# Norm sums on TensorE tile by tile, the scale spread from its column, and four column tiles per pass at the start of both attentions

## The chip, the cores and the metric

The kernel runs on one core of a Trainium2 chip. The metric is the time of one execution on the device in microseconds, lower is better. Three runs of the kernel before took 2327.4, 2330.2 and 2330.41 us, so its median is 2330.2 us. The profiled execution is a run of its own.

## The reference, cut to what matters

The model takes x of 512 positions by 1024 channels and runs three blocks after each other: a conformer convolution with a gated MLP, a differential attention with a gated MLP, and a block with two attention branches (a sparse one with top-k selection and a latent one) and an MLP. Only the norms and the products at their borders matter here.

```python
def rms_norm(x, g):
    y = x32 * lax.rsqrt(jnp.mean(x32 * x32, axis=-1, keepdims=True) + EPS)
    return (y * g.astype(jnp.float32)).astype(x.dtype)
...
h = rms_norm(x, norm_g[l, 0]) * (1.0 + sc_m) + sh_m
y = conformer_conv(h, ...)            # inside: layer_norm over channels
x = x + g_m * rms_norm(y, norm_g[l, 1])
h = rms_norm(x, norm_g[l, 2]) * (1.0 + sc_f) + sh_f
y = conv_ffn(h, ...)
x = x + g_f * rms_norm(y, norm_g[l, 3])
...
hkv = rms_norm(x, kv_norm_g)
k_shared, v_shared = hkv @ w_k, hkv @ w_v
```

A norm needs, for each position, the mean of squares over 1024 channels, its inverse root r, and then every channel of that position times r.

## The kernel before, in words

**Layout.** Channels lie on the 128 partitions and positions in the free dimension, so x is 8 tiles of 128x512 (`XT`). A mean over channels is a sum over partitions and over the 8 tiles. All large products are made of three products of split operands: `mm3` (L280 to L283) multiplies high by high, high by low and low by high. ScalarE makes the high part of an operand (a copy to fp32r), VectorE the low part (the difference).

**Weights.** `weight_plan` writes down every block of weights in order. A block is 128x1024 numbers (4 k tiles by 256 columns as a rule). SyncE loads it to one of 3 buffers `stg`, ScalarE makes `whi` (L308), VectorE `wlo` (L313). Three blocks can be split at a time: the split of block j waits until TensorE is done with block j - 3 (`gemm_done["block", j - NW]`). The function `next_block` does the splits up to two blocks ahead of the one that is used.

**Engines.** The program of each engine is written as one sequence; an instruction waits for semaphore counts, and engines work their sequences in order. `pe`, `act`, `dve`, `pool` and `sp` are TensorE, ScalarE, VectorE, GpSimd and SyncE. Small work is put between the steps of a product by generators: those in `within` get one turn after every two k steps of a product (8 turns for a product of two column tiles), and those in `beside` one at the end of each weight block.

**A norm, step by step.** `square` (L406) on ScalarE squares tile t into one of four buffers `sq`. `gather` (L411, L415) on GpSimd adds the squares of tiles 0 to 5 into `part`; a square t of 4 or more waits for the addition of t - 4. `sums8` on TensorE multiplies `part` and the squares of tiles 6 and 7 by a column of ones: each needs 4 products of a 128x128 weight by one column, and an fp32 product is two passes in the trace, so that is 3 x 8 = 24 passes into bank 6 (`NRM`). `begin_norm` on VectorE makes the variance (L437), waits for GpSimd's power (L447), and builds four 128x128 blocks of a diagonal of r (L442). `spread` on TensorE multiplies ones by this 128x512 diagonal, two passes into bank 7 (`SPREAD`), so that every partition has r of all positions. Then VectorE multiplies 8 tiles by it.

**Borders.** The norms are called by these names: `x` (start), `mean` and `ln` (LayerNorm of the convolution), `cy` (its output), `f0` and `fy0` (first MLP, before and after), `kv` (start of the first attention), `o0` to `o7` (heads), `ay` (its output), `f1`, `fy1` (second MLP), `z` (start of the last block), `cq` and `ckv` (its latents), `f2`, `fin`. At `x`, `ln`, `cy`, `f0`, `fy0`, `ay`, `f1`, `fy1`, `fin` nothing else is queued on TensorE between the norm and what follows. At `kv`, `z` and `f2` the product works on x times the gain before r is known: sums and spread stand within it, r is multiplied in when banks are evacuated, and bank 7 is first copied to SBUF (`RB`, L590).

**kv and z.** When the MLP before is done, VectorE adds its output to x tile by tile (`add_to_x_dve`: L499, L487) and makes the low part (L491); ScalarE makes the high part (L513) and the square. The first product (`w_k` or `z_ch`) runs beside this: two groups of two column tiles, each over 8 k tiles in two weight blocks. In group 0 TensorE takes 6 products per k tile. The sums stand at the end of group 0, the spread after 6 of the 16 steps of group 1. In z, tiles 0 to 2 of the result are latents with norms of their own (`latents_pe`, `latents_act`, `latents_dve`), and the fourth evacuation is followed by a rotation on VectorE and copies on ScalarE.

**The heads.** In the first attention TensorE's sequence mixes products of `w_q` and `w_o` with the scores, transposes and values of 32 items; once in four items a head's output is normed, with sums, power, diagonal and spread as above.

## Time and profile before

| | |
|---|---|
| runs | 2327.4, 2330.2, 2330.41 us |
| profiled execution, its own time | 2321.61 us |
| its span, first to last instruction | 2319.8 us |
| TensorE busy | 2108.7 us (91%) |
| weight loads busy | 1633.5 us (70%) |
| VectorE busy | 1421.7 us (61%) |
| ScalarE busy | 848.2 us (37%) |
| GpSimd busy | 119.1 us (5%) |
| mean granted clock of TensorE | 0.94 |

Busy time of TensorE counts modelled ends of pipelined products, so the start-to-start times of rows tell more than the sums. The granted clock is a share of 2.4 GHz: 1.00 is 2.4 and 0.50 is 1.2 GHz. The page's 40 slices of 58 us show the clock at 7 from `ln` to `f0` and at `ay` and `f1`, at 8 at `kv` and `z`, at 5 in the stretch from 1740 us in the last block, and at 9 nearly everywhere else. A time in the timeline is that of the first instruction of a merged row, `xN` their number.

### The profile page before, as it was taken

To read this page: it belongs to the slowest core of one execution; us is meant where nothing else is said; L and a number is where in the kernel's file an instruction comes from. 1 tells how busy PE (TensorE), PEld (TensorE's weight loads), DVE (VectorE), ACT (ScalarE), POOL (GpSimd) and SP (SyncE) were. 2 spreads that over 40 slices of the span, in tenths; PEclk is the share of its full clock that TensorE was granted. 3 is DMA by queue.
4 is the path that set the end of the run, shared out by engine and by line. 5 is a ranking of instruction groups with operands and counts; after the bars stand their busy time and mean duration, and the time that the engine had idled before them with its cause. 6 is when DMAs were issued, how large, how long until landed. Compare 5 with 4: busy or idle time off the path is not lost.

```text
span 2319.8 us, 25409 instructions
## 1 busy us (share of the span) xinstructions
PE 2108.7 (91%) x10180; PEld 1633.5 (70%) x10182; DVE 1421.7 (61%) x2430; ACT 848.2 (37%) x1397; POOL 119.1 (5%) x97
## 2 busy tenths in 40 slices
PE   3999769999998988886999999899889999999998
PEld 2655558888886875565888887677655588888886
DVE  6799768856845446646762563667767664633632
ACT  2333434433433245533442442423363433422331
POOL 1000120000011000011000001100000001000000
PEclk9999779999998999997999999899895899999999
DMA  7321235565531221011323222222110022332321
GB/s 281 112 73 37 101 108 192 196 201 173 196 103 55 72 65 37 28 47 32 108 92 103 96 87 95 70 82 69 32 37 2 1 83 90 100 93 90 105 94 64
DMA packets 61749, 214.74 MB, mean 93 GB/s; under 512 B 6848, under 2 KB 7744, under 8 KB 61632
## 3 DMA queue, kind: packets, MB, share of 16 engines
q1 hardware_dynamic: 61632, 213.12, 28.2%
q8 instruction: 80, 1.31, 0.2%
q14 instruction: 37, 0.30, 0.0%
HBM read 211.00 MB, written 2.10 MB: 92 GB/s over the span
## 4 chain that ended last, share of the span: by engine, by line
PE 78%; DVE 14%; ACT 3%; issue 2%; POOL 2%; DMA 1%; POOLq 0%; DVEq 0%; SPq 0%; ACTq 0%
PE bank L281 22%; PE bank L283 22%; PE bank L282 22%; PE bank L286 10%; DVE C L938 4%; PE bank L680 2%; DVE wlo L313 1%; POOL part L415 1%; DMA raw<-in_mod_w 1%; DVE raw L541 1%; DVE steps L733 1%; DVE tmp L499 1%; DVE Hl L491 1%; POOL small L447 1%; DVE tmp L462 1%
## 5 line engine op out<-in xcount | busy, mean ns | idle before, releaser
L281 PE MATMUL bank<-Hh,whi 128*128 128x512 f32 x1632 | 662.2, 406 | 72.4 <-DVE wlo L313 16.7
L282 PE MATMUL bank<-Hl,whi 128*128 128x512 f32 x1632 | 647.4, 397 | 0.0
L283 PE MATMUL bank<-Hh,wlo 128*128 128x512 f32 x1632 | 646.6, 396 | 0.0
L313 DVE TENSOR_TENSOR wlo<-stg,whi 128x1024 fp32r<-128x1024 f32 (+1 forms) x309 | 372.1, 1209 | 410.1 <-ACT whi L308 409.2
L308 ACT ACTIVATE whi<-stg 128x1024 fp32r<-128x1024 f32 (+1 forms) x309 | 314.0, 1026 | 448.6 <-PE bank L283 442.1
L281 PEld LDWEIGHTS bank<-Hh,whi 128*128 128x128 f32 x1632 | 313.7, 192 | 164.6 <-issue 37.5
L283 PEld LDWEIGHTS bank<-Hh,wlo 128*128 128x128 f32 x1632 | 313.7, 192 | 67.8
L282 PEld LDWEIGHTS bank<-Hl,whi 128*128 128x128 f32 x1632 | 314.5, 193 | 66.6 <-issue 3.4
L283 PE MATMUL bank<-HIDh,wlo 128*128 128x512 f32 x352 | 140.4, 399 | 0.0
L282 PE MATMUL bank<-HIDl,whi 128*128 128x512 f32 x352 | 138.7, 394 | 0.0
L281 PE MATMUL bank<-HIDh,whi 128*128 128x512 f32 x352 | 138.0, 392 | 0.0
L541 DVE CUSTOM_DVE_ANT_0 raw<-raw,c_act 128x1024 f32<-128x1024 f32 x96 | 117.6, 1230 | 18.2 <-DMA raw<-in_mod_w 18.0
L938 DVE SCALAR_TENSOR_TENSOR C<-U,vec,C 128x512 f32<-128x512 f32 x150 | 116.5, 776 | 4.9
L283 PE MATMUL bank<-HID2h,wlo 128*128 128x512 f32 x256 | 102.1, 399 | 0.0
L282 PE MATMUL bank<-HID2l,whi 128*128 128x512 f32 x256 | 100.9, 394 | 0.0
L281 PE MATMUL bank<-HID2h,whi 128*128 128x512 f32 x256 | 100.4, 392 | 0.0
L1219 DVE SCALAR_TENSOR_TENSOR tmp<-bank,vec,tmp 128x511 f32<-128x511 f32 x88 | 65.8, 748 | 50.3 <-ACT tmp L1182 50.3
L411 POOL TENSOR_TENSOR part<-sq 128x512 f32<-128x512 f32 x12 | 17.3, 1442 | 1457.1 <-ACT sq L406 1457.1
L1182 ACT ACTIVATE tmp<-bank,vec 128x512 f32<-128x512 f32 x88 | 67.8, 770 | 57.8 <-PE bank L283 57.8
L286 PE MATMUL bank<-U,dtap 128*128 128x512 f32 x186 | 81.0, 593 | 4.2 <-ACT dtap L1076 4.2
L282 PEld LDWEIGHTS bank<-HIDl,whi 128*128 128x128 f32 x352 | 66.1, 188 | 17.3
L281 PEld LDWEIGHTS bank<-HIDh,whi 128*128 128x128 f32 x352 | 66.1, 188 | 15.8
(284 smaller groups left out, 2625.6 us busy)
## 6 DMA issues: line engine op xcount, KB each, us to landing
raw<-in_mod_w SPq DMA_DIRECT2D x96, 512.0 KB, 4.6
stg<-in_ffn_in SPq DMA_DIRECT2D x88, 512.0 KB, 4.1
stg<-in_ff SPq DMA_DIRECT2D x64, 512.0 KB, 3.5
stg<-in_ffn_out SPq DMA_DIRECT2D x40, 512.0 KB, 3.6
stg<-in_cm_w SPq DMA_DIRECT2D x24, 512.0 KB, 4.4
stg<-in_gates SPq DMA_DIRECT2D x16, 512.0 KB, 3.5
stg<-in_z_ch SPq DMA_DIRECT2D x12, 512.0 KB, 3.5
stg<-in_w_k SPq DMA_DIRECT2D x8, 512.0 KB, 3.5
```

The costliest lines, as they stand in the source:

```text
L281: pe.e.matmul(out_, l[0], r[0], start=start, stop=False, skip_group_check=True)
L282: pe.e.matmul(out_, l[0], r[1], start=False, stop=False, skip_group_check=True)
L283: return pe.e.matmul(out_, l[1], r[0], start=False, stop=stop, skip_group_check=True)
L286: return pe.e.matmul(out_, l, r, start=start, stop=stop, skip_group_check=True)
L308: act.e.activation(whi[j % NW][:, 0:n * c], stg[j % NSTG][:, 0:n * c], ACT.Copy).then_inc(*w_hi.up(j))
L313: dve.e.tensor_tensor(wlo[j % NW][:, 0:n * c], stg[j % NSTG][:, 0:n * c], whi[j % NW][:, 0:n * c].bitcast(F32), ALU.subtract).then_inc(*w_ ...
L415: pool.e.tensor_tensor(part[:, :], part[:, :], sq[t % 4][:, :], ALU.add).then_inc(*pool_done.up(("gathered", s, t)))
L541: dve.e.tensor_tensor_reduce(raw[j % NRAW][:, :], raw[j % NRAW][:, :], c_act[:, :], 1.0, 0.0, ALU.mult, ALU.add, modv[:, a:a + 1]).then_in ...
L680: tok = pe.e.transpose(banks[b][:, kb * P:(kb + 1) * P], p[:, kb * P:(kb + 1) * P], ident[:, :])
L938: dve.e.scalar_tensor_tensor(C[:, t, :], U[:, t, k:k + S], vcol("cm_dw", 8 * k + t), C[:, t, :], ALU.mult, ALU.add).then_inc(*dve_done.up( ...
L1182: act.e.activation(at_, bank((("up", l, j), m))[:, :], ACT.Identity, bias=column(bcol + c), scale=column(w3 + 88 + c)).then_inc(*act_done. ...
L1219: dve.e.scalar_tensor_tensor(o[:, 1:S], from_[:, 0:S - 1], column(w3 + 44 + c), o[:, 1:S], ALU.mult, ALU.add).then_inc(*dve_done.up())
```

## The change

There are three parts, and what follows from them.

1. **Sums.** For the norms x, ln, f0, kv, f1 and z, GpSimd no longer adds squares. `one_sum` has TensorE multiply the square of one tile by ones, 8 passes, accumulating in bank 6 over 8 tiles; `sums_alone` calls it 8 times in a row (x, ln, f0, f1). A square of tile 4 or later waits for TensorE's sum of the tile four before. The norms cy, fy0, ay, fy1, f2 and fin keep GpSimd's additions and `sums8`.
2. **Spread.** The diagonal goes, and with it four (at ln eight) VectorE instructions per norm. `spread` takes column tb of r, repeated over 128 columns by a zero step, as the weight, and the identity as the moving operand: four products of 128 columns instead of one of 512. It waits for GpSimd's power, not for VectorE. VectorE's `begin_norm` no longer waits for the power.
3. **First products of kv and z.** `gemm_first` works on four column tiles in four banks at once: 12 products per k tile, then `one_sum` of that tile. Its weights come in four blocks of 2 k tiles by 512 columns. Banks rotate over six instead of five. The spread stands in the middle of the next group (tiles 4 and 5), where VectorE then evacuates four banks in a row. The latents of z begin in the group of tiles 6 and 7 instead of 4 and 5, with other counts of turns; ScalarE makes all three squares first. The bias tables of the first attention get four turns per weight block instead of three.

```diff
+    def first(name):
+        plan.extend((name, i, 2, 0, 512) for i in range(0, DT, 2))
...
-    gemm("w_k", 0, DT, range(0, D, 256))
+    first("w_k")
+    gemm("w_k", 0, DT, [512, 768])
...
+        ALONE = ("x", "ln", "f0", "kv", "f1", "z")
+
         def square(s, t, tile, ready):
             act.wait_ge(*ready)
             if t >= 4:
-                act.wait_ge(*pool_done["gathered", s, t - 4])
+                act.wait_ge(*(norm_done["part", s, t - 4] if s in ALONE else pool_done["gathered", s, t - 4]))
             act.e.activation(sq[t % 4][:, :], tile, ACT.Square).then_inc(*act_done.up(("sq", s, t)))
...
+        def one_sum(s, t):
+            if t == 0:
+                open_bank(NRM, [(dve_done, ("var", s))])
+            pe.wait_ge(*act_done["sq", s, t])
+            for tb in range(4):
+                tok = mm(banks[NRM][:, tb:tb + 1], sq[t % 4][:, tb * P:(tb + 1) * P], ones[:, 0:1], t == 0 and tb == 0, t == DT - 1)
+            tok.then_inc(*norm_done.up(("part", s, t), *([("sum", s)] if t == DT - 1 else [])))
+
+        def sums_alone(s):
+            for t in range(DT):
+                one_sum(s, t)
+
         def sums8(s):
             sums(s, [(part, pool_done["gathered", s, 5])] + [(sq[t % 4], act_done["sq", s, t]) for t in (6, 7)],
                  (dve_done, ("var", s)))
 
-        def begin_norm(s, count, power=True):
+        def begin_norm(s, count, eps=EPS):
             dve.wait_ge(*norm_done["sum", s])
-            dve.e.tensor_scalar(var4, banks[NRM][:, 0:4], 1.0 / count, EPS if power else 0.0, ALU.mult, ALU.add).then_inc(
-                *dve_done.up(("var", s)))
-            dve.wait_ge(*(pool_done["pow", s] if power else dve_done.now))
-            col = rs4 if power else var4
-            for tb in range(4):
-                dve.e.tensor_scalar(diag[:, tb * P:(tb + 1) * P], ident[:, :], col[:, tb:tb + 1], None, ALU.mult).then_inc(
-                    *dve_done.up(*([("diag", s)] if tb == 3 else [])))
+            dve.e.tensor_scalar(var4, banks[NRM][:, 0:4], 1.0 / count, eps, ALU.mult, ALU.add).then_inc(*dve_done.up(("var", s)))
 
         def power(s):
             pool.wait_ge(*dve_done["var", s])
             pool.e.tensor_tensor(rs4, var4, mhalf, ALU.pow).then_inc(*pool_done.up(("pow", s)))
 
-        def spread(s, by, where=SPREAD):
-            open_bank(where, by)
-            pe.wait_ge(*dve_done["diag", s])
-            mm(banks[where][:, :], ones[:, :], diag[:, :], True, True).then_inc(*norm_done.up(("spread", s)))
+
+        def spread(s, by, where=SPREAD, col=None, ready=None):
+            if by:
+                open_bank(where, by)
+            col = rs4 if col is None else col
+            pe.wait_ge(*(ready or pool_done["pow", s]))
+            for tb in range(4):
+                tok = mm(banks[where][:, tb * P:(tb + 1) * P], col[:, tb:tb + 1].to_broadcast([P, P]), ident[:, :], True, True)
+            tok.then_inc(*norm_done.up(("spread", s)))
...
+        def gemm_first(stage, name, s, by):
+            into = [acc_bank((stage, m), by(m)) for m in range(4)]
+            for i in range(0, DT, 2):
+                j = next_block(pe, name, i)
+                hi, lo = block_parts(j)
+                pe.wait_ge(*w_lo[j])
+                for q in range(2):
+                    xh, xl, ready = HX(s)(i + q)
+                    pe.wait_ge(*ready)
+                    for m in range(4):
+                        c = slice(m * P, (m + 1) * P)
+                        last = i + q == DT - 1
+                        tok = mm3(into[m][:, :], (hi[:, q, c], lo[:, q, c]), (xh, xl), i + q == 0, last)
+                        done = [(stage, m)] if last else []
+                        if q == 1 and m == 3:
+                            done.append(("block", j))
+                        if done:
+                            tok.then_inc(*gemm_done.up(*done))
+                    one_sum(s, i + q)
+
+        def beside_first(hand, name):
+            for i in range(0, DT, 2):
+                next_block(hand, name, i)
...
-        def first_pe(s):
-            for _ in range(7):
-                yield
-            sums8(s)
...
+        def first_pe(s, at=7, sums=sums8):
+            if sums:
+                for _ in range(at):
+                    yield
+                sums(s)
             for _ in range(3):
                 yield
             spread(s, [(act_done, ("rb", s))])
...
-                sums8("ln")
-                for d, key in ((diag, "lnr"), (diag2, "lne")):
-                    b = acc_bank(key, [(dve_done, ("lnb", DT - 1))])
-                    pe.wait_ge(*dve_done[key])
-                    mm(b[:, :], ones[:, :], d[:, :], True, True).then_inc(*norm_done.up(key))
+                sums_alone("ln")
+                for col, key, ready in ((rs4, "lnr", pool_done["lnpow"]), (er4, "lne", dve_done["er4"])):
+                    acc_bank(key, [(dve_done, ("lnb", DT - 1))])
+                    spread(key, None, bank_of[key], col, ready)
...
-                sums8(s)
+                sums_alone(s)
...
-                pe.within[:] = [first_pe("kv")]
-                for g in range(2):
-                    gemm("wk", "w_k", HX("kv"), 0, DT, 1, lambda m: [(dve_done, ("k", m))], 2 * g)
+                def by(m):
+                    return [(dve_done, ("k", m))]
+
+                rotate_banks([0, 1, 2, 3, 4, 5])
+                gemm_first("wk", "w_k", "kv", by)
+                pe.within[:] = [first_pe("kv", sums=None)]
+                gemm("wk", "w_k", HX("kv"), 0, DT, 1, by, 4)
                 pe.within[:] = []
+                rotate_banks([0, 1, 2, 3, 4])
                 tables = steps_pe("dt", 0, 16, Tb, [5])
-                pe.beside[:] = [tables] * 3
-                gemm("wk", "w_k", HX("kv"), 0, DT, 2, lambda m: [(dve_done, ("k", m))], 4)
+                pe.beside[:] = [tables] * 4
+                gemm("wk", "w_k", HX("kv"), 0, DT, 1, by, 6)
...
             def latents_pe():
                 for s, rows, _, _ in LATENTS:
-                    for _ in range(3):
-                        yield
-                    for x in rows[:-1]:
-                        yield
+                    yield
                     sums(s, [(sq[x], act_done["sq", s, x]) for x in rows], (dve_done, ("var", s)))
                     yield
                     yield
-                    yield
                     spread(s, [(dve_done, ("cqn", rows[-1]))], 5)
-                    yield
                     yield
 
             def latents_act():
@@ -1650,19 +1686,17 @@
                     for x in rows:
                         act.wait_ge(*dve_done["zt", x])
...
-                pe.within[:] = [first_pe("z")]
-                for g in range(2):
-                    gemm("z", "z_ch", HX("z"), 0, DT, 1, z_by, 2 * g)
+                rotate_banks([0, 1, 2, 3, 4, 5])
+                gemm_first("z", "z_ch", "z", z_by)
+                pe.within[:] = [first_pe("z", sums=None)]
+                gemm("z", "z_ch", HX("z"), 0, DT, 1, z_by, 4)
+                rotate_banks([0, 1, 2, 3, 4])
                 pe.within[:] = [latents_pe()]
-                gemm("z", "z_ch", HX("z"), 0, DT, 2, z_by, 4)
+                gemm("z", "z_ch", HX("z"), 0, DT, 1, z_by, 6)
```

`beside_first` makes the other engines take the same four blocks; `first_act` and `first_dve` get their place (`at`) and number of evacuations (`n`) as arguments.

## Rows read from the trace of the kernel before

**Rows 1.** The page, part 4: shares of the chain of waits by engine.
```profile
PE 78%; DVE 14%; ACT 3%; issue 2%; POOL 2%; DMA 1%; POOLq 0%; DVEq 0%; SPq 0%; ACTq 0%
```

**Rows 2.** TensorE's waits, whole span: us in total, times, longest.
```profile
PE bank L286 <- DVE diag L442: 29.4, 15, 6.9
...
PE bank L281 <- DVE Hl L491: 16.6, 9, 4.2
```

**Rows 3.** Timeline at border cy: start, us, engine, line, operation [idle before <-releaser].
```profile
310.95 0.88 DVE L442 TENSOR_SCALAR diag<-ident,small 128x128 f32<-128x128 f32 x4 [1.13 <-POOL small L447]
...
311.88 2.08 PE L286 MATMUL bank<-diag,ones 128*128 128x512 f32 x2 [2.26 <-DVE diag L442]
```

**Rows 4.** Timeline at borders f0 and f1, by engine.
```profile
328.81 3.55 PE L286 MATMUL bank<-ones,sq 128*128 128x1 f32 x16
...
315.39 0.69 DVE L487 TENSOR_TENSOR XT<-XT,tmp 128x512 f32<-128x512 f32 x1
...
319.17 1.10 DVE L487 TENSOR_TENSOR XT<-XT,tmp 128x512 f32<-128x512 f32 x1
...
316.11 0.63 ACT L406 ACTIVATE sq<-XT 128x512 f32<-128x512 f32 x1 [8.28 <-DVE XT L487]
...
1054.03 0.63 ACT L406 ACTIVATE sq<-XT 128x512 f32<-128x512 f32 x1 [7.67 <-DVE XT L487]
...
1066.12 3.55 PE L286 MATMUL bank<-ones,sq 128*128 128x1 f32 x16
```

**Rows 5.** TensorE's timeline at border ln.
```profile
237.63 1.87 PE L286 MATMUL bank<-ones,esum 128*128 128x1 f32 x8 [7.69 <-DVE esum L1021]
...
243.30 3.55 PE L286 MATMUL bank<-ones,sq 128*128 128x1 f32 x16
```

**Rows 6.** Windows: length, busy us (instructions) of PE, PEld, DVE, ACT, POOL; PEclk; DMA.
```profile
241.00:247.00 6.00, 5.28 (x24) 5.20 (x24) 0.04 (x1) 0.00 (x0) 0.52 (x1) 0.50 0.00 0
...
1745.00:1748.00 3.00, 3.00 (x54) 2.37 (x53) 2.96 (x10) 1.16 (x4) 0.00 (x0) 0.50 0.02 5
...
721.70:725.10 3.40, 2.10 (x8) 1.05 (x7) 3.40 (x4) 1.24 (x2) 2.60 (x2) 1.00 0.00 0
725.10:728.50 3.40, 0.94 (x3) 0.49 (x3) 3.40 (x4) 2.48 (x4) 1.70 (x1) 1.00 0.00 0
728.50:731.90 3.40, 3.18 (x8) 2.36 (x9) 2.64 (x6) 2.60 (x4) 0.00 (x0) 0.50 0.00 0
...
738.70:742.10 3.40, 3.40 (x10) 2.61 (x9) 2.01 (x5) 0.00 (x0) 0.43 (x1) 0.51 0.00 0
```

**Rows 7.** TensorE's timeline in the kernel's first product (cm_w1, four column tiles).
```profile
47.80 0.79 PE L281 MATMUL bank<-Hh,whi 128*128 128x512 f32 x1 [13.42 <-DVE wlo L313]
...
52.66 0.41 PE L283 MATMUL bank<-Hh,wlo 128*128 128x512 f32 x1
...
71.80 0.39 PE L283 MATMUL bank<-Hh,wlo 128*128 128x512 f32 x1
```

**Rows 8.** TensorE's timeline in the first product of kv.
```profile
715.26 0.77 PE L281 MATMUL bank<-Hh,whi 128*128 128x512 f32 x1 [4.18 <-DVE Hl L491]
...
735.91 1.93 PE L286 MATMUL bank<-ones,sq 128*128 128x1 f32 x16
...
751.22 0.39 PE L281 MATMUL bank<-Hh,whi 128*128 128x512 f32 x1
```

**Rows 9.** TensorE's timeline in the heads of the first attention.
```profile
894.18 1.12 PE L286 MATMUL bank<-diag,ones 128*128 128x512 f32 x2 [0.77 <-DVE diag L442]
...
897.63 1.06 PE L286 MATMUL bank<-aT,Vt 128*128 128x128 f32 x8
```

**Rows 10.** VectorE's timeline at the first norm.
```profile
31.37 0.88 DVE L442 TENSOR_SCALAR diag<-ident,small 128x128 f32<-128x128 f32 x4 [1.13 <-POOL small L447]
```

**Rows 11.** Timeline in z: fourth evacuation, and the squares of the latents.
```profile
1489.02 0.69 DVE L1965 TENSOR_TENSOR tmp<-bank,steps 128x512 f32<-128x512 f32 x1 [2.03 <-PE bank L283]
...
1494.55 1.14 ACT L1652 ACTIVATE sq<-VB 128x512 f32<-128x512 f32 x2
```

More of the change, by code:

```diff
@@ L119, in weight_plan @@
     ffn(1)
-    gemm("z_ch", 0, DT, [0, 256, 512, 768])
+    first("z_ch")
+    gemm("z_ch", 0, DT, [512, 768])
     gemm("z_ch", 0, DT, [1024, 1280])
@@ L584, in first_pe, with first_act @@
             spread(s, [(act_done, ("rb", s))])
-        def first_act(s, dst, evac=None):
-            for _ in range(10):
+        def first_act(s, dst, at=10, evac=None, n=2):
+            for _ in range(at):
                 yield
@@ L590, in first_act, with first_dve @@
             act.e.activation(dst, banks[SPREAD][:, :], ACT.Copy).then_inc(*act_done.up(("rb", s)))
-            for m in range(2 if evac else 0):
+            for m in range(n if evac else 0):
                 evac(m)
-        def first_dve(s, evac):
-            for _ in range(7):
+        def first_dve(s, evac, at=7, n=2):
+            for _ in range(at):
                 yield
@@ L600, in first_dve @@
             dve.wait_ge(*act_done["rb", s])
-            for m in range(2):
+            for m in range(n):
                 evac(m)
@@ L861, in gpsimd @@
                         *pool_done.up(("csum", i)))
-                pool.wait_ge(*norm_done["sum", "x"])
-                gather_six("ln")
                 pool.wait_ge(*dve_done["lnvar"])
@@ L913, in mean_of_early @@
                     sums("mean", [(csum, pool_done["csum", len(early) - 1])], (dve_done, ("var", "mean")))
-                conv_pe(CONV_PE[2], {17: mean_of_early, 23: lambda: spread("mean", [(dve_done, ("less", LAST[1]))])})
+                conv_pe(CONV_PE[2], {17: mean_of_early, 23: lambda: spread("mean", [(dve_done, ("less", LAST[1]))], SPREAD, var4, dve_done["var", "mean"])})
                 b = acc_bank("esum", [(dve_done, "e4")])
@@ L1008, in vector @@
                 next(convs)
-                begin_norm("mean", len(early) * P, power=False)
+                begin_norm("mean", len(early) * P, 0.0)
                 next(convs)
@@ L1033, in vector @@
                 dve.e.tensor_tensor(er4, e4, rs4, ALU.mult).then_inc(*dve_done.up("er4"))
-                for col, d, key in ((rs4, diag, "lnr"), (er4, diag2, "lne")):
-                    dve.wait_ge(*(norm_done["spread", "mean"] if d is diag else dve_done["er4"]))
-                    for tb in range(4):
-                        dve.e.tensor_scalar(d[:, tb * P:(tb + 1) * P], ident[:, :], col[:, tb:tb + 1], None, ALU.mult).then_inc(
-                            *dve_done.up(*([key] if tb == 3 else [])))
                 def low(t):
@@ L1043, in low @@
                         *dve_done.up(("h", "ln", t)))
-                dve.wait_ge(*norm_done["lnr"])
+                dve.wait_ge(*norm_done["spread", "lnr"])
                 for t in range(DT):
@@ L1473, in scalar @@
                 tables = steps_act("dt", 0, 16, lambda m: Bm[:, :, 256 + 64 * m:320 + 64 * m], [5])
-                act.beside[:] = [tables] * 3
-                beside_gemm(act, "w_k", 0, DT, 2)
+                act.beside[:] = [tables] * 4
+                beside_gemm(act, "w_k", 0, DT, 1)
                 def v_evac(g):
@@ L1533, in sync @@
             def sync():
-                for name in ("w_k", "w_v", "w_q"):
+                beside_first(sp, "w_k")
+                beside_gemm(sp, "w_k", 0, DT, 2)
+                for name in ("w_v", "w_q"):
                     beside_gemm(sp, name, 0, DT, 4)
@@ L1652, in latents_act @@
                         act.e.activation(sq[x][:, :], CQ[:, x, :], ACT.Square).then_inc(*act_done.up(("sq", s, x)))
-                    for _ in range(len(rows) + 6):
+                for s, rows, _, _ in LATENTS:
+                    for _ in range(4):
                         yield
@@ L1657, in latents_act @@
                         act.e.activation(CQh[:, x, :], CQ[:, x, :], ACT.Copy).then_inc(*act_done.up(("cqh", x)))
-                    yield
             def latents_dve():
                 for s, rows, gain_, n in LATENTS:
-                    for _ in range(len(rows) + 3):
-                        yield
+                    yield
                     begin_norm(s, n)
-                    yield
                     yield
```

48 lines of the change are left out of this document (23 added, 25 removed).

## The prediction

> **What bounds the kernel now.** I read the chain of waits first: 78% of it is TensorE, 14% VectorE [rows 1]. So only what shortens TensorE's queue, or what TensorE waits for, moves the end. The waits of TensorE come next [rows 2]: 29.4 us in 15 waits for the diagonal tile, 16.6 us in 9 for the split of the updated x at the start of the two attentions. Then I read the timeline at each border where a norm stands between two products. All borders have one shape: squares, column sums in bank 6, variance, power on GpSimd, four diagonal blocks on VectorE, one product with ones, and then VectorE works through eight tiles.
>
> **1. Diagonal gone, wide spread replaced by four narrow ones.** At the border after the first convolution VectorE builds the diagonal for 0.88 us after the power, and TensorE starts 0.93 us after that build started [rows 3]. The change starts TensorE at the power's end: -0.93 us wherever nothing else hides the chain: borders cy, f0, fy0, ay, f1, fy1, fin and the eighth head, 8 places, and about -1.0 at "ln". The narrow spread is not in the trace. It has 8 passes, each with its own weights. Nearest row at the high clock: 8 passes of 128 columns took 1.06 us, against 1.12 for a wide spread [rows 9]; at the low clock eight weight-bound passes of 0.22 [rows 5] and the last drain, some 2.1, against the wide 2.08 [rows 3]. I take 0; bounds -0.3 and +0.5 each, over some 18 exposed places -5 to +9.
>
> **2. Attention heads.** For each head VectorE waits for the power and builds the diagonal, and TensorE idles 0.77 us (0.68 in five others) before the spread [rows 9]. The power ends before TensorE's preceding products do, so this wait goes: 6 x 0.7 = -4.2. The eighth is in part 1. Bounds: 0, if the queues are held elsewhere, and -8, if VectorE's freed 2 us per head also remove later waits.
>
> **3. Start and mean.** At the start VectorE sat 1.13 us on the power and built for 0.88 [rows 10]; TensorE later waits for VectorE's weight split. VectorE would be 1.9 earlier, but the new spread ends some 2.1 after the power, which holds its first multiply: -1.3. The eight single sums end at about 26 us, before VectorE reads them at 30. The conv stage is dense on VectorE, so the mean's diagonal (again four blocks, 0.88) counts: -0.9. Bounds 0 and -3 together.
>
> **4. Single sums between stages (ln, f0, f1).** GpSimd's additions go, and TensorE does 8 tiles x 8 passes instead of 24 passes. What a tile costs depends on the clock. Sixteen passes took 3.55 us [rows 5], so 1.77 a tile, at a granted clock of 0.50, the 1.2 GHz level [rows 6]; at the high one 16 took 1.93, start to start 0.9 a tile [rows 8]. Would 14 us of such passes raise the clock? In the stretch at 1745 TensorE was 100% busy with narrow passes and the clock stayed at 0.50 [rows 6]; it did so from 1742 to 1784. I take low: 8 x 1.77 = 14.1 us.
> - ln: TensorE's sums stand behind the small sum that ends at 239.5. New end 239.5 + 14.1 = 253.6; now 243.30 + 3.55 = 246.9 [rows 5]: **+6.7**. Here the change loses: GpSimd had the work done while TensorE stood idle for VectorE.
> - f0: the first square ends at 316.11 + 0.63 = 316.7, so the sums end at 330.9, now 332.4 [rows 4]: -1.4. f1: 1054.7 + 14.1 = 1068.8, now 1069.7: -0.8.
> VectorE's additions took 1.10 us beside GpSimd against 0.69 alone [rows 4]; four of them get 0.4 faster, but TensorE, at 1.77 a tile, is behind VectorE's 1.3 a tile and hides it. The squares from tile 4 on now wait for the sum four tiles back: 7.1 us after the first, when that sum is long due.
>
> The Trainium skill has a rule that disagrees with the row. "TensorE: Matmul & The Clock Gate", section "LDWEIGHTS (loading the stationary operand)", gives a weight load as columns / 1.2, which does not depend on the granted clock. By it a tile would cost 8 x 0.107 = 0.85 us always and ln would lose nothing. The trace shows 0.22 a pass at the low clock and 0.11 at the high, so the row decides; the rule is kept as a rival.
>
> **5. First product of both attentions.** Now TensorE does 2 column tiles per k tile, waits for VectorE, and loses the clock after a stretch at 725 with 0.94 us of products in 3.4, and again, at 738, behind the sums [rows 6]. The first four tiles with sums and spread run from 715.26 to 751.22, 36.0 us [rows 8]. New: 12 products per k tile. The same order without sums stands in the first product of the kernel: from 47.80 to 71.80 + 0.23, 24.2 us for 96 products without a wait: 11 in the first 4.86 us, 0.44 each, then 85 at 0.23 [rows 7]. Add 8 sums x 0.9, the first rather at the low clock: 7.5, and the spread 0.9: 32.6. VectorE gives a split tile every 1.9 to 2.7 us; TensorE takes 3.6, so it is never starved after the first. The clock should hold once it is up: TensorE will be filled more densely with products than in the stretch at 721.7, which left it at 1.00 [rows 6]. Per attention 36.0 - 32.6 = -3.4, and -0.93 at the border (part 1). Queued behind: ScalarE's squares 4 to 7 wait for sums 0 to 3, the next high halves stand behind them, and after them the split of the fourth weight block. The last square comes about 17 us after the first product, that block is split at 19, needed at 24: hidden with 5 us to spare. If that cover goes, each us late costs one. The next block splits wait for the end of the four tiles; the evacuation of four banks is due before the bank it frees (12 us later).
> In "z" the latents' sums stand one group later in TensorE's order, but after 4 steps of it instead of 10, and VectorE has four evacuations to do ahead of them. Now the fourth evacuation starts at 1489.02, the rotation and copies follow, and the squares of the latents start at 1494.55, 5.5 us later [rows 11]. New: the fourth evacuation falls some 10 us after the group of tiles 4 and 5 starts, the squares end at 16, and TensorE asks for them at 14.6 (11.9 for the group, 2.7 for 12 products): +1.5. Bounds 0 and +4.
>
> The port that GpSimd and VectorE share is the other place to weigh: an L487 add 0.69 us alone, 1.10 beside GpSimd [rows 4]. The Trainium skill ("SBUF — State Buffer", section "Who interferes with whom") calls that an exclusive lock in which one fully waits for the other; the trace agrees in sign. By the rule alone f0 and f1 would gain 4 x 0.4 each; by the sum they gain it only if TensorE keeps up, which is the second rival.
>
> **Sum.** Diagonals 8 x -0.93 = -7.4, ln -1.0; heads -4.2; start and mean -2.2; ln +6.7, f0 -1.4, f1 -0.8; attentions 2 x -3.4 = -6.8; z +1.5. Together **-15.6 us**. The profiled execution took 2321.6 us (span 2319.8) and becomes 2306.0. The median of the runs shown, 2330.2, is 8.6 above it; the same difference gives **2314.6**, and that is the forecast.
>
> **Rivals.**
> - A, slower: the interleaved sums keep the clock at 0.50 in the first products of "kv" and "z". 96 products at 0.44 [rows 7] are 42.2, 8 sums 14.1: 56.3 instead of 31.7 before the spread, +24.6 per attention: in both 2364, in one 2339. It turns the sign once the low clock covers more than about a third of the two stretches beyond what I count. For it: 1.77 of sum after 5.1 of products at the low clock, and the fall behind the sums at 738. Against: the sparser stretch at 721.7 did not lower the clock [rows 6].
> - B, faster: a stream of sums at ln, f0 and f1 runs at the high rate, by a rise of the clock or because weight loads do not follow it. f0 and f1 would then end 0.9 after VectorE's last square, some 5 earlier each, ln some 5 to 7 earlier: 2297 to 2300. Against it stand rows 5 and 6.
> - C, the small gains do not carry: heads, start and mean give nothing because ScalarE's evacuations or another queue hold TensorE, and z's late squares cost 4: -15.6 + 6.4 + 2.5 = -6.7, 2323.5. For it: in the heads' stretch TensorE waits also for ScalarE's evacuations, which would take up what is freed. Against: VectorE's share of those waits shrinks as well.
>
> **How the numbers follow.** Forecast 0.52, A 0.12, B 0.12, C 0.24. What a measurement can tell from no change is about 0.2%, 4.7 us. Forecast and B are faster (0.64), C just over half (0.13): 0.77; of B's 0.12, 0.02 is for weight loads that do not follow the clock. Same: the rest of C and a mild A, 0.13. Slower 0.10. The range takes B's near side and most of C, with the spread's bounds: 2301 to 2328. The likeliest case's own range is 2307 to 2321.
>
> **What would show it.** No diagonal build; TensorE's spread right at the power's end. Sums at ln some 14 us long, at 0.50, ending 6.7 later after the small sum than now. From the first product of kv to the end of tile 3 some 32 us, clock 1.00 after the first 5, one tile each 3.6. In z a wait of TensorE for squares of about 1.5. Per head no wait before the spread. Wrong if the kv or z stretch takes over 36 us, if a tile's sum at ln takes 0.9, or if the time between the power and VectorE's first use of the spread exceeds 2.6.

## The result, and the profile after

The changed kernel took 2304.0 us (median of 4 runs, 2300.3 to 2306.8) beside 2328.8 (4 runs, 2324.8 to 2330.4) of the kernel before on the same chip: ratio 0.9895, 95% interval [0.9875, 0.9915]. Two later rounds, both on one chip, gave 0.9906 [0.9890, 0.9922] and 0.9907 [0.9885, 0.9928]. The forecast was 2314.6, range 2301 to 2328. The profiled executions are 2319.8 us of span before and 2298.5 after, so the traces have to explain 21.3 us; the working in the prediction came to 15.6.

TensorE's waits over the whole span (us in total, times, longest), to set against [rows 2]:

```profile
PE bank L286 <- DVE wlo L318: 25.1, 4, 14.3
PE bank L291 <- POOL small L461: 17.4, 9, 6.2
PE bank L291 <- ACT sq L414: 16.7, 3, 10.9
PE bank L291 <- DVE steps L778: 12.3, 7, 2.7
PE bank L286 <- DVE Hl L510: 8.4, 2, 4.2
```

The diagonal is gone; what is left of that wait ends with GpSimd's power. The waits for Hl are halved (16.6 to 8.4), as expected. Two things were not expected: the wait for the low half of the weights grew from 16.7 to 25.1 us, and the 8.4 us wait for Vt, which the kernel before had once, is missing.

The timeline of TensorE at cy and f0 (start us, length us, engine, line, operation; in brackets the idle time before and what ended it), against [rows 3, 4]:

```profile
314.09 1.73 PE L291 MATMUL bank<-ident,small 128*128 128x128 f32 x8 [1.35 <-POOL small L461]
318.75 13.78 PE L291 MATMUL bank<-ones,sq 128*128 128x1 f32 x64 [2.92 <-ACT sq L414]
333.96 2.04 PE L291 MATMUL bank<-ident,small 128*128 128x128 f32 x8 [1.43 <-POOL small L461]
```

The idle time at a border is 1.35 instead of 2.26 us: -0.91. The 64 passes of f0 take 13.8 us.

The same engine at ln, and the granted clock beside it (window, length, then busy time of each engine, PEclk, DMA share, GB/s), against [rows 5]:

```profile
235.95 1.87 PE L291 MATMUL bank<-ones,esum 128*128 128x1 f32 x8 [7.04 <-DVE esum L1061]
237.68 13.79 PE L291 MATMUL bank<-ones,sq 128*128 128x1 f32 x64
253.11 3.64 PE L291 MATMUL bank<-ident,small 128*128 128x128 f32 x16 [1.64 <-POOL small L907]
```
```profile
238.00:252.00 14.00, 13.47 (x64) 13.39 (x63) 0.52 (x4) 3.80 (x5) 0.00 (x0) 0.50 0.01 2
```

From 237.7 to 251.5: 13.8 us at a granted clock of 0.50 with TensorE busy throughout. The Trainium skill ("TensorE: Matmul & The Clock Gate", section "LDWEIGHTS (loading the stationary operand)") has a formula without the clock in it, by which the 64 weight loads of this stretch would take an estimated 0.107 us each. At 0.50 the trace has 13.8 / 64 = 0.22 a pass, so the rule does not hold at the low level. Nor did the clock rise in this stretch, so both ways to rival B are out.

The first product of kv:

```profile
713.47 0.76 PE L286 MATMUL bank<-Hh,whi 128*128 128x512 f32 x1 [4.18 <-DVE Hl L510]
718.08 0.95 PE L291 MATMUL bank<-ones,sq 128*128 128x1 f32 x8
721.75 0.95 PE L291 MATMUL bank<-ones,sq 128*128 128x1 f32 x8
732.96 0.50 PE L286 MATMUL bank<-Hh,whi 128*128 128x512 f32 x1 [2.92 <-DVE wlo L318]
737.10 1.26 PE L291 MATMUL bank<-ones,sq 128*128 128x1 f32 x8
748.39 0.95 PE L291 MATMUL bank<-ones,sq 128*128 128x1 f32 x8
```
```profile
718.00:733.00 15.00, 12.08 (x71) 10.37 (x69) 8.44 (x14) 7.39 (x11) 0.00 (x0) 1.00 0.00 0
733.00:738.00 5.00, 5.00 (x18) 4.12 (x19) 2.18 (x2) 0.54 (x1) 0.00 (x0) 0.66 0.78 240
```

A tile is done every 3.67 us at clock 1.00, as forecast (3.6), so rival A is out too. But after four tiles TensorE waits 2.92 us for a low half of the weights, and works at 0.66 of the clock for the 5 us behind it. What held that half is on ScalarE and VectorE:

```profile
722.74 0.64 ACT L414 ACTIVATE sq<-XT 128x512 f32<-128x512 f32 x1 [1.62 <-PE bank L291]
726.41 0.63 ACT L414 ACTIVATE sq<-XT 128x512 f32<-128x512 f32 x1 [2.42 <-PE bank L291]
730.07 0.63 ACT L414 ACTIVATE sq<-XT 128x512 f32<-128x512 f32 x1 [2.42 <-PE bank L291]
730.61 2.94 ACT L313 ACTIVATE whi<-stg 128x1024 fp32r<-128x1024 f32 x3
```
```profile
731.68 3.50 DVE L318 TENSOR_TENSOR wlo<-stg,whi 128x1024 fp32r<-128x1024 f32 x3 [3.17 <-ACT whi L313]
```

The squares wait for TensorE's sums four tiles back, the split of the weights stands behind the last square. In z it is the same, and there VectorE has conversions of positions (L2014 to L2020) and the steps behind them ahead of its split as well:

```profile
1429.22 0.76 PE L286 MATMUL bank<-Hh,whi 128*128 128x512 f32 x1 [4.18 <-DVE Hl L510]
1451.14 0.79 PE L286 MATMUL bank<-Hh,whi 128*128 128x512 f32 x1 [4.88 <-DVE wlo L318]
1466.57 0.95 PE L291 MATMUL bank<-ones,sq 128*128 128x1 f32 x8
```

And here is the wait that the change removed without being meant to. First TensorE, then ScalarE, in the kernel *before*, ahead of the query product:

```profile
843.85 0.79 PE L281 MATMUL bank<-Hh,whi 128*128 128x512 f32 x1 [8.42 <-ACT Vt L1481]
847.43 0.63 PE L283 MATMUL bank<-Hh,wlo 128*128 128x512 f32 x1
848.39 0.40 PE L283 MATMUL bank<-Hh,wlo 128*128 128x512 f32 x1
```
```profile
841.62 0.72 ACT L474 ACTIVATE Hh<-tmp,modv 128x512 fp32r<-128x512 f32 x1 [0.60 <-DVE tmp L462]
842.25 1.55 ACT L1481 ACTIVATE Vt<-bank,small 128x256 f32<-128x256 f32 x4
```

The query product starts in banks 0 and 1. The last value tile of the kernel before lay in bank 0 (sixteen tiles in a rotation of five, counted on from the stage ahead), and its evacuation stands on ScalarE behind the eight high halves of the query's input. The changed kernel restarts its rotation after six key tiles; its last value tiles lie in banks 3 and 4.

Lengths between the starts of GpSimd's powers, read from the traces (us; "narrow" is the experiment with the narrow spread alone, below):

```
                              before   after    diff  forecast | narrow
start to power x               30.32   29.84    -0.5      0.0  |   -1.1
x to ln                       217.09  222.19    +5.1     +4.5  |   -1.5
ln to cy                       62.49   60.99    -1.5     -1.0  |   +0.2
cy to f0                       22.74   19.79    -3.0     -2.3  |   -0.9
f0 to fy0                     374.38  373.33    -1.1     -0.9  |   -0.9
fy0 to o0                     185.19  169.77   -15.4     -4.3  |   -3.4
o0 to ay (the heads)          155.61  150.74    -4.9     -5.1  |   -6.4
ay to f1                       22.13   20.09    -2.0     -1.7  |   -0.9
f1 to fy1                     375.02  375.15    +0.1     -0.9  |   -0.7
fy1 to f2                     516.66  519.30    +2.6     -2.8  |   -4.4
f2 to end                     358.17  357.31    -0.9     -0.9  |   -0.9
```

The forecast's -1.3 for the start stands in the second row, since its diagonal comes behind the power of x. Nine rows lie within 1.1 us of the forecast. Two do not, and they have opposite signs: "fy0 to o0" gained 11.1 more, "fy1 to f2" lost 5.4 more. A row of one execution carries some noise: in the two later profiles of the changed kernel the rows lie within 1.5 us of these, but for the heads, where one of them has 154.7.

### The profile page after: what moved, and what is told of

Same layout as the page of the kernel before. It is cut to its first block, busy times and chain, and to the rows that moved or that the text cites. A ratio compares the mean times of both kernels' runs of the same rounds, so it can differ in the third digit from the quotient of the medians.

```text
span 2298.5 us, 26045 instructions
## 1 busy us (share of the span) xinstructions
PE 2140.2 (93%) x10564; PEld 1691.6 (74%) x10566; DVE 1385.5 (60%) x2334; ACT 848.5 (37%) x1397; POOL 74.7 (3%) x67
## 4 chain that ended last, share of the span: by engine, by line
PE 81%; DVE 12%; ACT 3%; issue 2%; DMA 1%; POOL 0%; POOLq 0%; DVEq 0%; SPq 0%; ACTq 0%
PE bank L286 23%; PE bank L288 22%; PE bank L287 22%; PE bank L291 12%; DVE C L979 4%; PE bank L725 2%; DMA raw<-in_mod_w 1%; DVE wlo L318 1%; DVE steps L778 1%; DVE raw L560 1%; ACT pr L698 1%; DVE Hl L486 0%; ACT whi L313 0%; DVE tmp L481 0%; DVE sc L1776 0%
## 5 line engine op out<-in xcount | busy, mean ns | idle before, releaser
L286 PE MATMUL bank<-Hh,whi 128*128 128x512 f32 x1632 | 656.0, 402 | 64.4 <-DVE wlo L318 25.1
L291 PEld LDWEIGHTS bank<-ones,sq 128*128 128x128 f32 x568 | 94.6, 257 | 20.2 <-issue 10.9
L291 PE MATMUL bank<-ones,sq 128*128 128x1 f32 x568 | 93.2, 294 | 17.5 <-ACT sq L414 16.7
```

The source lines that it names most:

```text
L286: pe.e.matmul(out_, l[0], r[0], start=start, stop=False, skip_group_check=True)
L291: return pe.e.matmul(out_, l, r, start=start, stop=stop, skip_group_check=True)
```

## Experiments

Each ran against the kernel before on one chip, and runs under one heading shared it, but for the pair at the end of the first heading. The changed kernel itself ran beside the others only in that pair and under the second heading; elsewhere two ratios are compared across chips. The theory after the traces: (a) the early stage gained by a bank collision that went away, and by table steps that start later; (b) the new product order gained nothing, because a weight split is late in both attentions; (c) ln lost what was forecast. The rivals are that these waits are only exchanged for others.

### Banks, the late split, and ln

Banks, in the kernel before:

```diff
+                rotate_banks([2, 0, 1, 3, 4])
                 pe.within[:] = [first_pe("kv")]
```

> Kernel before with one line more: the accumulator banks of the key and value products rotate as 2, 0, 1, 3, 4, so that the last pair of value tiles lies in banks 4 and 2 instead of 4 and 0, and the query product (banks 0 and 1) finds both free. Theory (bank collision): TensorE's 8.4 us wait for Vt at 843 goes, and with it the low clock of the first nine query products (0.43 instead of 0.23 us each, 1.8): 8.5 + 1.7 = 10.2 us faster than before, ratio 0.9956, no wait of TensorE for Vt in the trace. Rival (a queue holds it: VectorE and ScalarE are busy with the eight tiles of the query input in that stretch and TensorE would wait for a split of those or of a weight block instead): at most 3 us faster, and a wait for Hl or wlo at 835 to 843.

Measured 0.9949 [0.9932, 0.9965], 12 us faster. In its trace the 8.4 us wait is gone and none has taken its place before the query product. One line, in the kernel before, gives half of what the whole change gives.

The collision put back into the changed kernel:

```diff
-                rotate_banks([0, 1, 2, 3, 4])
+                rotate_banks([2, 3, 4, 0, 1])
                 tables = steps_pe("dt", 0, 16, Tb, [5])
```

> Changed kernel, with the five banks after the sixth key tile rotated as 2, 3, 4, 0, 1, so that the last pair of value tiles lies in banks 0 and 1, as one of the pair did before. Theory (bank collision): a wait of about 8 us for Vt comes back ahead of the query product, with the low clock behind it: 10 us slower than the changed kernel, so about 15 us faster than before (ratio 0.9936) instead of 25. Rival (the wait of before came from something else, for instance from the tables that stood one group earlier): the same time as the changed kernel within 2 us.

Measured 0.9965 [0.9952, 0.9978]: 8 us faster than before instead of 22 to 24, so the collision costs 14 to 16 by the runs, more than the 10 expected; in the traces "fy0 to o0" is 180.9 instead of 169.8 us, the rest is spread over other stages. TensorE's timeline:

```profile
841.91 0.76 PE L286 MATMUL bank<-Hh,whi 128*128 128x512 f32 x1 [8.47 <-ACT Vt L1521]
```

By this run the change would have been worth 8 us without the accident; by the 12 us that the banks gave alone, 10 to 13.

The split of the third block moved ahead of the squares that wait (`presplit` with `split + 1` splits one more block):

```diff
                     scale_high(s, t, then, used)
+                    if t == 4:
+                        presplit(act, act.split + 1)
...
                 low(DT - 2)
+                presplit(dve, dve.split + 1)
                 low(DT - 1)
```

> Changed kernel, in which ScalarE and VectorE split the third weight block of both attentions among the updates of x (ScalarE behind the fifth high half, VectorE ahead of the last low half) instead of behind all squares. Theory (the split stands behind squares that wait for sums): the waits of 2.9 us in kv and 4.9 us in z for the low half of the weights go, and with them the slower products behind them (the fifth tile took 4.1 and 4.4 us instead of 2.8): 2.9 + 1.3 + 4.9 + 1.7 = 10.8 us faster than the changed kernel, 35 to 36 us faster than before, ratio 0.9848; the stretch to the end of tile 7's sum 31.6 us in both. Rival (TensorE only waits for the next thing, the squares or the fourth block): at most 3 us faster than the changed kernel.

Measured 0.9879 [0.9861, 0.9898]: 4 to 7 us faster than the changed kernel's 0.9895 to 0.9907, where 10.8 were expected, and the intervals overlap, so this run alone does not show a gain. The local part is right. TensorE in kv and z, first product and last sum of the four tiles:

```profile
717.21 0.77 PE L286 MATMUL bank<-Hh,whi 128*128 128x512 f32 x1 [4.18 <-DVE Hl L510]
748.11 0.95 PE L291 MATMUL bank<-ones,sq 128*128 128x1 f32 x8
...
1431.74 0.77 PE L286 MATMUL bank<-Hh,whi 128*128 128x512 f32 x1 [4.18 <-DVE Hl L510]
1462.11 0.95 PE L291 MATMUL bank<-ones,sq 128*128 128x1 f32 x8
```

No wait is left in either stretch, and they are 31.9 and 31.3 us long to the end of the eighth sum (31.6 expected; 35.9 and 38.3 in the changed kernel). From power to power, "fy0 to kv" is 4.6 us shorter and "fy1 to z" 7.0. But this execution, the slowest of its five, has a span of 2298.7 us beside the changed kernel's 2298.5: all of it was given back behind the two places that the edit mends. "ln to cy" took 1.7 us more, "kv to o0" 1.6, the heads 2.8, the last block behind its latents 2.2, and "f2 to fin" 348.8 instead of 346.1. The ten microseconds from f2's power, first in this kernel, then in the changed one:

```profile
1939.00:1949.00 10.00, 10.00 (x38) 8.09 (x37) 2.22 (x3) 1.09 (x2) 1.87 (x1) 0.73 0.15 54
```
```profile
1941.00:1951.00 10.00, 10.00 (x49) 8.36 (x49) 4.22 (x7) 2.21 (x4) 1.93 (x1) 1.00 0.18 54
```

TensorE is busy throughout in both; at 0.73 of the clock it gets through 38 matmuls, at 1.00 through 49.

ln on GpSimd again:

```diff
-        ALONE = ("x", "ln", "f0", "kv", "f1", "z")
+        ALONE = ("x", "f0", "kv", "f1", "z")
...
+                gather_six("ln")
                 pool.wait_ge(*dve_done["lnvar"])
...
-                sums_alone("ln")
+                sums8("ln")
```

> Changed kernel, in which the squares of ln are again added by GpSimd (six tiles, then two by TensorE) and TensorE makes 24 passes there instead of 64. Theory (narrow passes at the low clock cost 1.77 us a tile and stand on the path): 14.1 us of sums become 5.3 behind a wait of about 2, so 6 to 7 us faster than the changed kernel, 31 us faster than before, ratio 0.9866. Rival (the gathered sums wait for GpSimd and VectorE slows beside it): within 2 us of the changed kernel.

Measured 0.9890 [0.9872, 0.9907], which could not be told from the changed kernel on another chip, though the stretch from the small sum to ln's spread was 10.9 instead of 17.2 us. So it ran again beside the changed kernel:

> The changed kernel again, as the yardstick of the run beside it: ratio to before 0.9895 to 0.9906.

> The changed kernel with the squares of ln added by GpSimd, once more and now beside the changed kernel on one chip. Theory (the stretch from the small sum to ln's spread, 17.2 us in the changed kernel and 10.9 in this one, stands on the path and carries): 5 to 6 us faster than the changed kernel. Rival (later dips of the clock give it back, as the first run, 0.9890, left possible): within 2 us.

Measured 0.9907 [0.9885, 0.9928] for the changed kernel and 0.9868 [0.9847, 0.9888] for this one: medians 2303.4 and 2296.3, 7.1 us apart, and every run of one is below every run of the other. The traces agree once several are taken: from the power of x to that of cy, the five profiles with ln's sums on TensorE took 282.9 to 285.4 us, the six with GpSimd's additions and the narrow spread 277.3 to 278.9, on the mean 6.0 less. The forecast's +6.7 stands.

### Narrow spread alone, late tables, both mends

> The changed kernel once more, as the yardstick of the other runs on this chip: ratio 0.9895 as measured before; the variants of the changed kernel that ran on another chip (early split 0.9879, ln gathered 0.9890) are to be compared with what it gives here.

It gave 0.9906 [0.9890, 0.9922], median 2301.7.

The narrow spread alone, in the kernel before (`begin_norm` without the diagonal, `spread` as in the change, everything else as it was):

> Kernel before with the narrow spread alone: no diagonal builds, all squares still added by GpSimd, products in their old order, banks as before. Theory (the prediction's parts 1 to 3): eight borders 7.4, ln 1.0, heads 4.2, mean 0.9 and at the start 0.5 (what the trace after shows in place of 1.3): 14.0 us faster than before, ratio 0.9940; no wait of TensorE for diagonals, 1.4 for the power at each border, the border after the first convolution 0.9 shorter. Rival (the freed VectorE time in the heads carries nothing): 9 to 10 us faster, 0.9960.

Measured 0.9905 [0.9890, 0.9920], median 2302.2: 21 us faster than before, where 14 were expected, and no slower than the whole change beside it. The bank collision is still in it (8.4 us for Vt). The column "narrow" above shows where: the borders as worked out; 3.4 instead of 0.9 in "fy0 to o0", 6.4 instead of 5.1 in the heads, 4.4 instead of 0.9 in "fy1 to f2". In the heads TensorE's waits differ from the kernel before's by the diagonal alone (6.5 us, of which 1.4 stay for the power), in "fy1 to f2" by under 1 us beyond the border's. So no wait explains the 7 us beyond the forecast; what does differ is the mean granted clock, 0.948 instead of 0.940, and not all of it comes back: a later kernel with the same code in "fy1 to f2" took 515.2 us there, 1.4 less than before, where this one took 4.4 less. TensorE's fourth stall in z, before and then with the narrow spread:

```profile
1466.66 0.80 PE L281 MATMUL bank<-Hh,whi 128*128 128x512 f32 x1 [1.91 <-DVE Hl L491]
```
```profile
1449.68 0.50 PE L281 MATMUL bank<-Hh,whi 128*128 128x512 f32 x1 [1.91 <-DVE Hl L489]
```

The stall has the same length, the product behind it takes 0.80 us in one and 0.50 in the other: behind the first the clock was down, behind the second it was not. Why an earlier border leads there was not tried by itself and stays open.

The table steps one group later, in the kernel before with the banks mended:

```diff
+                gemm("wk", "w_k", HX("kv"), 0, DT, 1, lambda m: [(dve_done, ("k", m))], 4)
-                pe.beside[:] = [tables] * 3
-                gemm("wk", "w_k", HX("kv"), 0, DT, 2, lambda m: [(dve_done, ("k", m))], 4)
+                pe.beside[:] = [tables] * 4
+                gemm("wk", "w_k", HX("kv"), 0, DT, 1, lambda m: [(dve_done, ("k", m))], 6)
```

> Kernel before with the banks rotated as in the first experiment and, in addition, the table steps begun one group of two key tiles later, as in the changed kernel (four turns in the last group instead of three and three). Theory (the stretch from the end of the first four key tiles to the first value product was 35.0 us long before and 29.9 after because four waits for the steps tables, 4.6 us, and the low clock behind them became two waits): 5 us faster than the banks alone, 17 us faster than before, ratio 0.9927, that stretch 30 to 31 us. Rival (the steps only move into the value products and cost there what they cost before): the same as the banks alone, 0.9949.

Measured 0.9923 [0.9907, 0.9939], 6 us on top of the banks, though on another chip and with intervals that overlap; "fy0 to o0" 165.0 instead of 172.5 us. TensorE's waits from 700 to 860 hold one for the steps, where the kernel before had four of 4.6 us together:

```profile
PE bank L286 <- DVE steps L733: 1.5, 1, 1.5
```

Together the two accidents, banks and tables, are worth 18 us in the kernel before.

The changed kernel with the early split and ln on GpSimd:

> Changed kernel with both mends: the third weight block of both attentions split early, and the squares of ln added by GpSimd. Theory (both terms carry, 10.8 and 6.3 us of stretches that the profiles showed shorter): 17 us faster than the changed kernel beside it, ratio to before 0.9822. Rival (shorter waits are given back by dips of the granted clock in later stretches, which the profile of the early split showed as 2 to 3 us in several places): half of it, 8 us faster than the changed kernel, 0.986.

Measured 0.9847 [0.9828, 0.9867], median 2291.8: 10 us faster than the changed kernel by the medians, 14 by the ratios, between rival (8) and theory (17). Its "f2 to fin" is again 348.9 us.

### Is the product order worth anything?

> Kernel before with the narrow spread, the banks rotated as in the first experiment, the table steps one group later, and the squares of f0 and f1 summed tile by tile; ln, kv and z keep GpSimd's additions, and both attentions their old product order of two tiles per pass. Theory (the parts add up: narrow spread 22.1 by the runs, banks and tables 17.9, f0 and f1 about 2): 42 us faster than before, ratio 0.9819. Rival (the changed kernel's product order is worth what the prediction said, so that leaving it out costs 3.4 us per attention against the mended kernel): no better than the changed kernel with both mends, 0.9847.

Measured 0.9859 [0.9843, 0.9876], median 2289.2. It stays 9 us short of the sum, so the parts do not add. In the profiles 4.9 of that is in "fy0 to o0" (3.4 by the narrow spread alone and 20.2 by banks and tables, 18.8 together), 2.0 in the heads and 2.4 in "fy1 to f2". The stage "fy0 to o0" is 166.4 us, the same as with the new order, the early split and interleaved sums (166.5), and "fy1 to f2" 515.2 against 516.1. With 64 passes of sums among the products, no gain of the new order over the old can be seen, even mended; the two runs are on different chips, and a difference of some 3 us could hide.

The new order without interleaved sums:

```diff
-                    one_sum(s, i + q)
+            sums8(s)
```

> The changed kernel with both mends, but in kv and z the squares are added by GpSimd as before and TensorE makes its 24 passes of sums once, behind the first product of four tiles. Theory (the interleaved sums cost 8 x 0.8 = 6.5 us per attention on a TensorE that is never starved there, the gathered ones 2.6): 3.9 us less in each, first four tiles 28 to 29 us, 8 us faster than with interleaved sums, ratio 0.981. Rival (VectorE beside GpSimd gives a tile every 2.7 us on the mean, TensorE takes 2.8, waits and loses the clock): within 2 us of it, 0.984 to 0.985.

Measured 0.9831 [0.9816, 0.9846], median 2281.4, the fastest of all: 39 us faster than the kernel before, 6 to 8 faster than the old order beside it. Between theory (0.981) and rival (0.984) its interval does not decide. The trace shows part of the theory's gain, and another wait than the rival's. TensorE in kv and then in z:

```profile
709.59 0.76 PE L286 MATMUL bank<-Hh,whi 128*128 128x512 f32 x1 [4.18 <-DVE Hl L510]
725.49 0.79 PE L286 MATMUL bank<-Hh,whi 128*128 128x512 f32 x1 [2.16 <-DVE wlo L318]
...
1420.35 0.76 PE L286 MATMUL bank<-Hh,whi 128*128 128x512 f32 x1 [4.18 <-DVE Hl L510]
1436.26 0.50 PE L286 MATMUL bank<-Hh,whi 128*128 128x512 f32 x1 [2.57 <-DVE wlo L318]
1448.13 1.93 PE L291 MATMUL bank<-ones,sq 128*128 128x1 f32 x16
```

From the first product to the end of the sums it is 31.2 us in kv and 29.7 in z, instead of 31.3 and 32.1 with interleaved sums. TensorE never waits for a split tile after the first, which was the rival's reason, but the third block is late again in both. Without the sums TensorE asks for it sooner, in kv 13.7 us after the first product instead of 16.5. And VectorE has it ready later, at 15.9 instead of 12.5: beside GpSimd's additions three of its splits up to there took 1.78 us instead of 0.74. So what the rival named is at work, at another place.

The stage "fy0 to o0" gains only 1.0 (165.5). "fy1 to f2" is 509.0 instead of 516.1 us, of which 3.1 lie behind the power of z, where the kernel with both mends took 474.8 and this one 471.6. But five of the six profiles of the new order with the late split have 471.8 to 472.2 there and the sixth 474.3, so that part is a step of the clock. "f2 to fin" is back at 346.1 us, which is luck of the clock as well and no merit of this kernel.

## Why the prediction was right, and where it was not

**Direction right, and the mechanism of parts 1, 2 and 4; total too small, part 5 wrong, and two large errors that partly cancel.** The sum said -15.6, the profiles show -21.3, the runs -22 to -25. The forecast of 2314.6 was 10.6 us too high: 5.7 by the sum, and the other 4.9 because it took over the 8.6 us between the profiled execution and the median of three runs, which for the changed kernel were 3.7.

- **1, diagonals, -0.93 at 8 borders and -1.0 at ln: right.** The idle time went from 2.26 to 1.35 us; the narrow spread took 1.7 to 2.1 at the low clock (the wide one 2.08), so 0 for it was right. At "f1 to fy1" the gain is missing in this execution; the narrow spread alone shows -0.7 there, a second profile of the changed kernel -0.9.
- **2, heads, -4.2 and the eighth's 0.93: right** (-4.9 in all), and no head's spread waits any more. Of the 11 profiles with the narrow spread, nine have 149.2 to 151.0 us from o0 to ay and two have 153.6 and 154.7; the three with the diagonal have 155.2 to 155.6. Rival C is out.
- **3, start -1.3: too much.** The first product starts at 47.25 instead of 47.80, -0.5, and that half microsecond is there already at the power of x, ahead of the diagonal: the term itself gave nothing. VectorE's freed time met missing data (it waited 0.56 and 1.19 us for the modulation's rows from DMA). The narrow spread alone starts at 46.20, of which again 1.1 are there before the power.
- **4, single sums: right.** ln +6.6 by the row "x to ln" (+5.1 against the narrow spread's -1.5), 6.0 with the row behind it and over all profiles, 7.1 by the runs; f0 and f1, with the narrow spread's own gain taken off, -2.1 and -1.1 (forecast -1.4 and -0.8).
- **5, kv and z, -3.4 each: wrong.** The pace (3.67 a tile) and the clock were right; the cover was not. "That block is split at 19, needed at 24": it was split at 19.5, but it was the third block, not the fourth, and needed at 16.5. A block of the new plan holds two column pairs of two k tiles instead of one pair of four, so TensorE is through two blocks after four tiles. "If that cover goes, each us late costs one" was right and still low: 2.9 us late cost 4.0 in kv and 4.9 cost 7.0 in z (the four tiles' length without the stall, in the early split), with the clock down behind each stall. The four tiles with the spread's 0.8 took 36.5 and 39.0 us instead of 32.6. The prediction had named this sign itself, wrong if either stretch takes over 36, and it came up in both: the gain of 3.4 per attention was not there.
- **z's latents, +1.5:** 0.47 us of wait.
- **What the prediction did not see at all:** the bank collision (8.5 us of idle and 1.5 of low clock) and the later tables (5.1), both in "fy0 to o0". The row was there to be read: a wait of TensorE for Vt, 8.4 us, stood in the waits of the kernel before. The change rewrites the rotation of banks ahead of it, and part 5 looked no further than the fourth tile.

Taking the narrow spread alone (-20.8 us by its profile) from the whole change (-21.3) leaves -0.5 for parts 4 and 5 with both accidents in them. The sum said -0.8 for the same parts (its +6.7, -2.2, -6.8, +1.5). That the two agree is luck, within steps of the clock of some 3 us; the content is not right: it is ln's loss and two late splits, paid for by a bank and a table. And the narrow spread gave 21 us where the sum had 14.8 for it; the rest of that is open.

## What to carry to other kernels

When an edit changes how many tiles pass through a rotation of buffers, write down which buffer every later owner gets, up to the next place where the rotation restarts, and hold it against the waits of the profile: a wait of 8 us hung on an index modulo five. When the shape of the weight blocks changes, count in blocks, not in tiles, when each is needed, and look at what stands ahead of its split on each in-order queue. And measure the parts of a bundled change alone: here one part alone gave as much as the whole, another lost 7 us, and undoing that one, moving one split and regrouping the sums took the kernel from 0.990 to 0.983.

## What the runs showed of the hardware

- VectorE beside GpSimd can pay more than the add of [rows 4] showed (0.69 to 1.10 us). First VectorE in kv before, then GpSimd there, then VectorE in kv after, where GpSimd is idle:

```profile
716.30 1.77 DVE L491 SCALAR_TENSOR_TENSOR Hl<-XT,vec,Hh 128x512 fp32r<-128x512 f32 x1
717.99 0.73 DVE L499 SCALAR_TENSOR_TENSOR tmp<-Yf,gains,bank 128x512 f32<-128x512 f32 x1
```
```profile
715.88 1.64 POOL L411 TENSOR_TENSOR part<-sq 128x512 f32<-128x512 f32 x1 [7.84 <-ACT sq L406]
717.74 1.48 POOL L415 TENSOR_TENSOR part<-part,sq 128x512 f32<-128x512 f32 x1 [0.22 <-ACT sq L406]
```
```profile
716.43 0.74 DVE L510 SCALAR_TENSOR_TENSOR Hl<-XT,vec,Hh 128x512 fp32r<-128x512 f32 x1
```

  The split took 1.77 us and ended 0.55 behind GpSimd's addition. In the last experiment's kv three more splits and two adds that met an addition took 1.78 and 1.11 to 1.12 us, and each ended 0.54 to 0.56 behind it, whenever it had begun. That fits the exclusive lock of the Trainium skill ("SBUF — State Buffer", section "Who interferes with whom"), as far as GpSimd's spans can be trusted. The operation after the split above, whose second input is a bank, ran in 0.73 us with GpSimd at work beside it: that one waited for nothing.
- The same products over 346 us ("f2 to fin", where only the spread's form differs) came out at 346.1 us in 10 of the 14 profiled executions of this study and at 348.8 or 348.9 in the other 4, and the heads from o0 to o7 between 114.8 and 120.3, the latter not looked into; of the former one pair was compared, and the granted clock at its start was the difference. A local gain of 3 us can vanish in such a step, or look doubled; stage tables from several executions show it, one total does not.
